# Four more weight remainders on GpSimd, idle products before the first ones, layer norm sums added on Vector, and one key join moved up

## The chip, the cores and the metric

The kernel runs on one core of a Trainium2 chip. TensorE multiplies, Vector and Scalar (rows: DVE and ACT) do the elementwise work, GpSimd (POOL) does some of it, and SyncE (SP) issues nearly all transfers. The metric is the device time of one execution in microseconds.

## The reference

Two transformer blocks of width 2048 on one sequence of 256 tokens, in float32. The change lies in the first half of the first block:

```python
h = rms_norm(x, mix_norm_g)
proj = h @ w_in
q, kv, gate_logits, conv_in = jnp.split(proj, splits, axis=-1)
attn = nsa_attention(q, kv, gates, ...)        # compressed, selected and window branches
# conformer_conv:
a, gate = jnp.split(conv_in, 2, axis=-1)
u = a * jax.nn.sigmoid(gate)
u = causal_depthwise_conv(u, conv_w, conv_b)   # 31 taps, 1024 channels
u = layer_norm(u, ln_g, ln_b)                  # mean and variance over the 1024 channels
conv = jax.nn.silu(u)
x = x + jnp.concatenate([attn, conv], axis=-1) @ w_out
```

Behind it come a gated feed-forward layer with a convolution, and a second block (latent attention, gated linear attention, feed-forward), which the change leaves alone.

## The kernel before

**Products and weights.** Every float32 number a is taken apart as a_hi + a_lo (a_hi rounded for TensorE's fast float32 format), and a product is w_hi*h_hi + w_hi*h_lo + w_lo*h_hi. A planner (`make_plan`) cuts all weights into chunks of 128 x 1024 numbers (512 KB) in the order of use. SyncE loads chunks into 7 raw slots; Scalar rounds a chunk to w_hi (L1193); Vector subtracts to make the remainder w_lo (L1675); TensorE multiplies. w_hi and w_lo have 4 slots, so a chunk can be rounded when the products of the fourth chunk before it are through, and a raw slot is loaded again when the remainder is made. `p.pool_rate` gives the remainders of a stretch of chunks to GpSimd (L2473): from the fifth chunk up to the fourth query tile. `lead(i)` is the third chunk behind chunk i: Scalar and Vector go on rounding and subtracting up to there (`round_until`, `rests_until`) before they turn to the result of the tile that ends in chunk i.

**Order of work.** Each engine has one program, written out by hand, and works it off in order; semaphores tie them together. Scalar squares the rows of x (two tiles of 128 tokens), GpSimd makes the factor of each row (L2477, L2480), and Vector scales x by it in quarters of 512 columns (L1695: quarter 0 of both token tiles, quarter 1 of both, quarters 2 and 3 ahead of k=2 and k=6 of the next step). For each k of 16, TensorE transposes two blocks (L711), Scalar makes h_hi (L1225), and Vector h_lo (L1732). The first pair of tiles, `conv_first`, consists of four chunks of four k's each: for each k two hi products of 512 columns (L617), and at the end of a chunk its eight w_lo products of 256 columns (L618). Transposes run four k's ahead of products.

**Tiles.** 128 output columns each: 16 of the convolution's input, 4 of the compressed keys and values, 8 queries, the gates (48 columns), 4 keys: (1,0), (1,1), (2,0), (2,1); then the value group (two k's for each chunk). A tile's low half is copied out by Scalar (`split_low`, L1258), and Vector adds it (`join_low`, `join_scaled`, L1845). Below, chunks are named by what they hold: K6 holds the last six pieces of key (2,0) and the first two of (2,1), V0, V1 and V2 are the first three of the values.

**Convolution and its layer norm.** Vector runs the 31 taps of eight channel tiles, two tiles at a time (`conv_taps`, L1793, L1796), in portions between its other work: `taps(n)` does the next n instructions, and what is left when the queries are joined is done then. The norm needs sums over 1024 channels, which is eight tiles of 128 partitions: TensorE adds them all with a matrix of ones, eight products on conv_y behind the gates (L811) and eight on the squares behind the tile of key (1,1) (L819). Between the two sums Scalar makes the mean (behind the rounding of chunk K6, L1292), Vector centres (L1887), Scalar squares (L1295). Then follow the root, its refinement, the scaling by it, Scalar's swish (L1312), rounding to mix_hi and the rest mix_lo. The first attention scores (L833) wait for key (2,1), whose join on Vector stands behind the remainders of V1 and V2:

```python
def join_scaled(key, i, dst, scale, done_sem):
    rests_until(lead(final[key]))
    w.wait_ge(low_split, i + 1)
```

TensorE's side of the two sums:

```python
for j in range(CONV_TILES):
    w.wait_ge(taps_done, j + 1)
    t = e.matmul(banks[7][:, 0:T], ones, conv_y[:, j, :], start=j == 0, stop=j == CONV_TILES - 1)
```

`keep_busy` issues products whose result nobody reads, so that TensorE doesn't stand idle while x is normed; it does so ahead of the second, third and fourth h, not of the first.

Of the kernel before, what the change touches and what calls it, by code (L numbers as in the profile page):

```python
# [137 lines left out]
def make_plan():  # L138
# [3 lines left out]
    conv = gates + N_BRANCH * HEADS  # L142
    p.project_pair("conv_first", ("conv_a", 0), ("conv_g", 0), "w_in", (conv, conv + CONV_CH), P)
    p.pool_rate = 1.0
# [151 lines left out]
def two_blocks(nc, WEIGHTS, X, PARAMS, PARAMS1, PARAMS2, POSITIONS, COND, FINAL_ROW, OUT):  # L296
# [12 lines left out]
    with ctx:  # L309
# [122 lines left out]
        low = place("low", "mid", 0, [P, 2, T])  # L432
        sig = place("sig", "mid", (KD + KD // 2) * T * 4 + 2048, [P, 2, T])
# [57 lines left out]
        IDLE_PRODUCTS = ((0, 0), (10, 0), (15, 5), (17, 4))  # L491
# [5 lines left out]
        def sem(name):  # L497
            return ctx.enter_context(nc.semaphore(name))
# [21 lines left out]
        low_split, low_joined = sem("low_split"), sem("low_joined")  # L520
        pads_ready, conv_g_ready, conv_in, taps_done = sem("pads_ready"), sem("conv_g_ready"), sem("conv_in"), sem("taps_done")
# [60 lines left out]
        def tensor_program(e):  # L582
# [112 lines left out]
            def keep_busy(stage, number):  # L695
                if number:
                    src = (None, mix_hi, ff_hi, mix_hi)[stage]
                    b = (None, 5, 2, 2)[stage]
                    fill(b)
                    for _ in range(number):  # L700
                        e.matmul(banks[b][:, :], src[:, 0, 0:P], src[:, 0:2, :].rearrange("p k t -> p (k t)"), start=True, stop=True)
# [34 lines left out]

            w.wait_ge(gains_landed, 16)
# [46 lines left out]
            wide_tile("gates", need, (gates_T_ready, 1), NG)  # L784
            def compressed_scores():
# [22 lines left out]
            fill(7)  # L808
            for j in range(CONV_TILES):
                w.wait_ge(taps_done, j + 1)  # L810
                t = e.matmul(banks[7][:, 0:T], ones, conv_y[:, j, :], start=j == 0, stop=j == CONV_TILES - 1)  # L811
            t.then_inc(ln_summed, 1)
            free[7] = ln_mean_ready, 1
            for at_key, (br, j) in enumerate(((1, 1), (2, 0), (2, 1))):
                if at_key == 1:
                    fill(7)
                    for i in range(CONV_TILES):
                        w.wait_ge(squared, i + 1)
                        t = e.matmul(banks[7][:, 0:T], ones, ln_sq[:, i, :], start=i == 0, stop=i == CONV_TILES - 1)  # L819
                    t.then_inc(ln_summed, 1)  # L820
                    free[7] = ln_var_ready, 1
# [1901 lines left out]
```

## Time and profile before

| | |
|---|---|
| time, median of 3 runs | 2220.71 us (2220.49 to 2220.9) |
| the profiled execution's own time | 2220.59 us |
| its span | 2218.8 us |
| TensorE busy | 2188.2 us (99%) |
| Vector busy | 1574.1 us (71%) |
| Scalar busy | 1123.3 us (51%) |
| GpSimd busy | 128.3 us (6%) |

Busy time of TensorE is the time from the start of a matmul to its modelled end; matmuls overlap, so the spacing of their starts says what one costs. In the timeline a row stands for one or several equal instructions in a row (x8); its first number is the start of the first in us from the span's start, its second the time to the end of the last. What stands in square brackets is how long the engine had been idle and what ended that.

### The profile page before, as it was taken

The numbers are of one execution on the slowest core, as the hardware profiler recorded it, in microseconds if no ns is written. First come the engines' busy times: TensorE is split into PE (matmuls) and PEld (weight loads), VectorE is DVE, ScalarE is ACT, GpSimd is POOL, SyncE is SP. The second block draws the span as 40 slices with busy tenths as digits, with TensorE's granted clock in tenths as the row PEclk, the third lists the DMA queues.
The fourth block names the chain that finished last, engine by engine and source line by source line (L and its number), as shares of the span: only waits on it lengthen the run. The fifth ranks groups of instructions, "written<-read, shape, count | busy, mean of one in ns | idle before, by whom it ended". The sixth has DMA issues, their size and how long they took to land.

```text
span 2218.8 us, 29547 instructions
## 1 busy us (share of the span) xinstructions
PE 2188.2 (99%) x11637; PEld 1853.1 (84%) x11637; DVE 1574.1 (71%) x2417; ACT 1123.3 (51%) x1683; POOL 128.3 (6%) x92
## 2 busy tenths in 40 slices
PE   7999999999999999999999999999999999999998
PEld 6888787888888888888889887878888888888986
DVE  5896886899998799998875665576555555544455
ACT  5444775555543455554455656554444444444443
POOL 5850000000000000000000000000000000000000
PEclk9999999999999999999999999999999999999999
DMA  7754436788899888889955551647676776655563
GB/s 265 225 190 149 135 99 207 245 291 286 292 313 369 308 281 289 290 286 373 338 169 180 177 175 55 233 140 248 230 221 227 227 233 233 214 192 189 182 214 118
DMA packets 139915, 504.00 MB, mean 227 GB/s; under 512 B 15616, under 2 KB 18048, under 8 KB 138880
## 3 DMA queue, kind: packets, MB, share of 16 engines
q1 hardware_dynamic: 138960, 496.85, 67.0%
q0 software_dynamic: 528, 3.16, 0.4%
q8 instruction: 92, 1.51, 0.3%
q10 hardware_dynamic: 288, 2.10, 0.3%
q14 instruction: 47, 0.39, 0.1%
HBM read 499.54 MB, written 2.51 MB: 226 GB/s over the span
## 4 chain that ended last, share of the span: by engine, by line
PE 84%; DVE 12%; ACT 2%; issue 1%; DMA 0%; POOL 0%; POOLq 0%; SPq 0%; DVEq 0%; ACTq 0%
PE bank L627 20%; PE both L627 18%; PE bank L617 13%; PE bank L630 10%; PE both L630 9%; PE bank L618 7%; DVE w_lo L1675 5%; DVE raw L1657 2%; PE bank L620 1%; PE bank L622 1%; PE bank L621 1%; ACT ffn_g L1403 1%; ACT ffn_a L1397 1%; PE bank L876 1%; PE both L833 1%
## 5 line engine op out<-in xcount | busy, mean ns | idle before, releaser
L1675 DVE TENSOR_TENSOR w_lo<-raw,w_hi 128x1024 fp32r<-128x1024 f32 x693 | 840.7, 1222 | 449.7 <-ACT w_hi L1193 448.3
L1193 ACT ACTIVATE w_hi<-raw 128x1024 fp32r<-128x1024 f32 x737 | 767.7, 1054 | 616.2 <-PE bank L630 295.2
L617 PE MATMUL bank<-h_both,w_hi 128*128 128x512 f32 x1936 | 495.0, 395 | 2.8 <-DVE h_both L1732 2.8
L617 PEld LDWEIGHTS bank<-h_both,w_hi 128*128 128x128 f32 x1936 | 346.1, 189 | 66.0 <-DVE h_both L1732 4.4
L618 PEld LDWEIGHTS bank<-h_both,w_lo 128*128 128x128 f32 x1936 | 264.7, 190 | 19.1
L618 PE MATMUL bank<-h_both,w_lo 128*128 128x256 f32 x1936 | 272.2, 283 | 0.0
L1657 DVE SCALAR_TENSOR_TENSOR raw<-raw,silu_c 128x1024 f32<-128x1024 f32 x192 | 234.0, 1219 | 0.0
L627 PE MATMUL bank<-w_hi,h_both 128*128 128x512 f32 (+2 forms) x1024 | 233.9, 372 | 0.0
L627 PE MATMUL both<-w_hi,h_both 128*128 128x512 f32 (+1 forms) x960 | 228.4, 379 | 1.4 <-DVE h_both L1752 1.4
L627 PEld LDWEIGHTS bank<-w_hi,h_both 128*128 128x128 f32 x1024 | 181.9, 188 | 33.1 <-issue 0.7
L627 PEld LDWEIGHTS both<-w_hi,h_both 128*128 128x128 f32 x960 | 169.3, 188 | 33.9 <-DVE h_both L1752 2.8
L630 PE MATMUL bank<-w_lo,h_both 128*128 128x512 f32 (+2 forms) x512 | 126.4, 371 | 0.0
L630 PE MATMUL both<-w_lo,h_both 128*128 128x512 f32 (+1 forms) x480 | 120.7, 375 | 0.0
L627 PE MATMUL bank<-w_hi,ff_hi 128*128 128x512 f32 x352 | 111.0, 389 | 0.0
L627 PE MATMUL bank<-w_hi,ff_lo 128*128 128x512 f32 x352 | 110.9, 389 | 0.0
L627 PE MATMUL both<-w_hi,ff_hi 128*128 128x512 f32 x352 | 108.7, 390 | 1.0 <-ACT w_hi L1193 1.0
L627 PE MATMUL both<-w_hi,ff_lo 128*128 128x512 f32 x352 | 108.4, 389 | 0.0
L2473 POOL TENSOR_TENSOR w_lo<-raw,w_hi 128x1024 fp32r<-128x1024 f32 x44 | 104.9, 2408 | 39.6 <-ACT w_hi L1193 38.7
L630 PEld LDWEIGHTS bank<-w_lo,h_both 128*128 128x128 f32 x512 | 91.4, 188 | 16.2
L630 PEld LDWEIGHTS both<-w_lo,h_both 128*128 128x128 f32 x480 | 86.3, 188 | 16.4
L630 PE MATMUL bank<-w_lo,ff_hi 128*128 128x512 f32 x352 | 95.4, 389 | 0.0
L630 PE MATMUL both<-w_lo,ff_hi 128*128 128x512 f32 x352 | 94.1, 389 | 0.0
(369 smaller groups left out, 2343.9 us busy)
## 6 DMA issues: line engine op xcount, KB each, us to landing
raw<-weights SPq DMA_DIRECT2D x924, 512.0 KB, 4.5
raw<-weights SPq DMA_DIRECT2D x5, 504.0 KB, 7.3
x<-x SPq DMA_DIRECT2D x2, 1024.0 KB, 5.8
bias<-bias_rows SPq DMA_DIRECT2D x8, 256.0 KB, 6.8
silu_c<-c ACTq DMA_DIRECT2D x2, 1024.0 KB, 4.7
gate_row<-gate_rows POOLq DMA_DIRECT2D x2, 1024.0 KB, 9.0
out<-x SPq DMA_DIRECT2D x8, 256.0 KB, 2.7
final_row<-final_row POOLq DMA_DIRECT2D x1, 1024.0 KB, 5.2
```

What stands on the lines that cost most here:

```text
L617: return e.matmul(out, hi, a_both[:, k, :, :].rearrange("p a t -> p (a t)"), start=first, stop=last)
L618: return e.matmul(out[:, 0:T], lo, a_hi[:, k, :], start=False, stop=False)
L620: e.matmul(out, hi, a_hi[:, k, :], start=opens and first, stop=False)
L621: return e.matmul(out, hi, a_lo[:, k, :], start=False, stop=False)
L622: return e.matmul(out, lo, a_hi[:, k, :], start=False, stop=closes and last)
L627: t = e.matmul(outs[o], stationary[:, k, o * P:(o + 1) * P], hi, start=opens and first and stationary is a_hi, stop=False)
L630: t = e.matmul(outs[o], a_hi[:, k, o * P:(o + 1) * P], lo, start=False, stop=closes and last)
L833: t = e.matmul(both[:, side, br * n:(br + 1) * n], queries[r, j, tt * P:(tt + 1) * P], keys[r, br, j // GQA, 0:n], start=True, stop=True)
L1193: e.activation(w_hi[:, n % PART_SLOTS, 0:widths[i]], raw[:, i % RAW_SLOTS, 0:widths[i]], ACT.Copy).then_inc(hi_ready, 1)
L1657: e.scalar_tensor_tensor(src, src, 1.0, silu_c[:, half, :], ALU.mult, ALU.mult, accum_out=ada_parts[:, v, kt, half:half + 1]).then_inc(ada ...
L1675: e.tensor_tensor(w_lo[:, slot, 0:widths[i]], raw[:, i % RAW_SLOTS, 0:widths[i]], w_hi[:, slot, 0:widths[i]].bitcast(F32), ALU.subtract).t ...
L2473: e.tensor_tensor(w_lo[:, slot, 0:widths[i]], raw[:, i % RAW_SLOTS, 0:widths[i]], w_hi[:, slot, 0:widths[i]].bitcast(F32), ALU.subtract).t ...
```

## The change

Four parts. (1) `pool_rate` is set before the first chunk, so GpSimd makes the remainders of chunks 0 to 3 as well; Vector makes none of them. (2) Vector clears a small tile, `blank`, and TensorE runs 8 products on it at once, 10 when the first half of x has landed, 5 between the first two transposes, and 2 when the first four k's are transposed. (3) Vector adds the eight tiles of conv_y, and later the eight tiles of squares, into one tile of 256 columns (ln_q); TensorE then needs one product with the matrix of ones for each sum. The first seven additions are put into `conv_taps`, behind each pair of channel tiles; the second seven stand behind the centring and the remainder of the next chunk, K6. (4) Scalar splits and Vector joins key (2,1) before the last chunks of its lead (V1 and V2) are subtracted (on Scalar: before V2 is rounded).

```diff
     conv = gates + N_BRANCH * HEADS
+    p.pool_rate = 1.0
     p.project_pair("conv_first", ("conv_a", 0), ("conv_g", 0), "w_in", (conv, conv + CONV_CH), P)
-    p.pool_rate = 1.0
     for j in range(1, CONV_TILES):
...
         low = place("low", "mid", 0, [P, 2, T])
+        blank = place("blank", FR, 0, [P, 512], BF16)
         sig = place("sig", "mid", (KD + KD // 2) * T * 4 + 2048, [P, 2, T])
...
         WITH_H = (WITH_PAIR, WITH_PAIR, WITH_GROUP, WITH_GROUP)
-        IDLE_PRODUCTS = ((0, 0), (10, 0), (15, 5), (17, 4))
+        WARM_PRODUCTS = (8, 10)
+        IDLE_PRODUCTS = ((5, 2), (10, 0), (15, 5), (17, 4))
         TURN_BANKS = ((6, 7, 0, 1), (6, 7, 0, 1), (6, 7, 4, 5), (6, 7, 4, 5))
...
                 if number:
-                    src = (None, mix_hi, ff_hi, mix_hi)[stage]
-                    b = (None, 5, 2, 2)[stage]
+                    b = (2, 5, 2, 2)[stage]
                     fill(b)
                     for _ in range(number):
-                        e.matmul(banks[b][:, :], src[:, 0, 0:P], src[:, 0:2, :].rearrange("p k t -> p (k t)"), start=True, stop=True)
+                        if stage == 0:
+                            e.matmul(banks[b][:, :], blank[:, 0:P], blank[:, :], start=True, stop=True)
+                        else:
+                            src = (mix_hi, ff_hi, mix_hi)[stage - 1]
+                            e.matmul(banks[b][:, :], src[:, 0, 0:P], src[:, 0:2, :].rearrange("p k t -> p (k t)"), start=True, stop=True)
 
...
 
+            w.wait_ge(dve_step, 1)
+            keep_busy(0, WARM_PRODUCTS[0])
+            w.wait_ge(x_landed[0], 16)
+            keep_busy(0, WARM_PRODUCTS[1])
             w.wait_ge(gains_landed, 16)
...
             wide_tile("gates", need, (gates_T_ready, 1), NG)
+            def norm_sum(added, taken):
+                w.wait_ge(norm_added, added)
+                fill(7)
+                e.matmul(banks[7][:, 0:T], ones, ln_q[:, :], start=True, stop=True).then_inc(ln_summed, 1)
+                free[7] = taken, 1
+
             def compressed_scores():
...
                 free[2 + tt] = gates_ready, tt + 1
-            fill(7)
-            for j in range(CONV_TILES):
-                w.wait_ge(taps_done, j + 1)
-                t = e.matmul(banks[7][:, 0:T], ones, conv_y[:, j, :], start=j == 0, stop=j == CONV_TILES - 1)
-            t.then_inc(ln_summed, 1)
-            free[7] = ln_mean_ready, 1
+            norm_sum(1, ln_mean_ready)
             for at_key, (br, j) in enumerate(((1, 1), (2, 0), (2, 1))):
                 if at_key == 1:
-                    fill(7)
-                    for i in range(CONV_TILES):
-                        w.wait_ge(squared, i + 1)
-                        t = e.matmul(banks[7][:, 0:T], ones, ln_sq[:, i, :], start=i == 0, stop=i == CONV_TILES - 1)
-                    t.then_inc(ln_summed, 1)
-                    free[7] = ln_var_ready, 1
+                    norm_sum(2, ln_var_ready)
                 wide_tile(("key", br, j), need, (keys_ready, at_key + 2))
...
             for at_key, (br, j) in enumerate(((1, 1), (2, 0), (2, 1))):
-                split_low(made(("key", br, j)), 30 + at_key, ((low_joined, 21), (keys_ready, 1), (keys_ready, 2))[at_key])
+                if at_key == 2:
+                    round_until(final["key", br, j])
+                    w.wait_ge(multiplied, done_at["key", br, j])
+                    split_low(banks[bank_of["key", br, j]], 32, (keys_ready, 2))
+                    round_until(lead(final["key", br, j]))
+                else:
+                    split_low(made(("key", br, j)), 30 + at_key, ((low_joined, 21), (keys_ready, 1))[at_key])
                 if at_key == 0:
...
 
+            chain(e.memset(blank[:, :], 0.0))
             for parts, value in ((out1_parts, D * EPS), (final_parts, D * EPS), (product_parts, 0.0), (o2_raw_parts, D * EPS),
...
             def conv_taps():
-                before = {}
+                before, last_tap = {}, {}
                 for j0 in range(0, CONV_TILES, 2):
...
                                 if j >= 2:
-                                    w.wait_ge(taps_done, j - 1)
+                                    w.wait_ge(dve_step, last_tap[j - 2])
                                 before[j] = chain(e.tensor_scalar(so_far, u, tap_w, conv_b[:, j:j + 1], ALU.mult, ALU.add))
...
                                 w.wait_ge(dve_step, before[j])
-                                e.scalar_tensor_tensor(conv_y[:, j, :], u, tap_w, so_far, ALU.mult, ALU.add).then_inc(taps_done, 1)
+                                last_tap[j] = chain(e.scalar_tensor_tensor(conv_y[:, j, :], u, tap_w, so_far, ALU.mult, ALU.add))
                             yield
+                    w.wait_ge(dve_step, last_tap[j0 + 1])
+                    if j0 == 0:
+                        so_far_y = chain(e.tensor_tensor(ln_q[:, :], conv_y[:, 0, :], conv_y[:, 1, :], ALU.add))
+                        yield
+                        continue
+                    for j in (j0, j0 + 1):
+                        w.wait_ge(dve_step, so_far_y)
+                        t = e.tensor_tensor(ln_q[:, :], ln_q[:, :], conv_y[:, j, :], ALU.add)
+                        if j < CONV_TILES - 1:
+                            so_far_y = chain(t)
+                        else:
+                            t.then_inc(norm_added, 1)
+                        yield
 
...
             def join_scaled(key, i, dst, scale, done_sem):
-                rests_until(lead(final[key]))
+                rests_until(lead(final[key]) if i < 32 else final[key])
                 w.wait_ge(low_split, i + 1)
...
             for j in range(CONV_TILES):
-                w.wait_ge(taps_done, j + 1)
                 e.tensor_tensor(conv_y[:, j, :], conv_y[:, j, :], ln_mean[:, :], ALU.subtract).then_inc(centred, 1)
+            rests_until(lead(final["key", 1, 0]) + 1)
+            w.wait_ge(squared, 2)
+            t = chain(e.tensor_tensor(ln_q[:, :], ln_sq[:, 0, :], ln_sq[:, 1, :], ALU.add))
+            for j in range(2, CONV_TILES):
+                w.wait_ge(squared, j + 1)
+                w.wait_ge(dve_step, t)
+                if j < CONV_TILES - 1:
+                    t = chain(e.tensor_tensor(ln_q[:, :], ln_q[:, :], ln_sq[:, j, :], ALU.add))
+                else:
+                    e.tensor_tensor(ln_q[:, :], ln_q[:, :], ln_sq[:, j, :], ALU.add).then_inc(norm_added, 1)
             rests_until(lead(final["key", 1, 1]))
...
             join_scaled(("key", 2, 1), 32, keys[:, 1, 1, :], 1.0, keys_ready)
+            rests_until(lead(final["key", 2, 1]))
             for j in range(CONV_TILES):
```

## Rows read from the trace of the kernel before

**Rows 1.** The page, chain that ended last: shares of the span by engine.
```profile
PE 84%; DVE 12%; ACT 2%; issue 1%; DMA 0%; POOL 0%; POOLq 0%; SPq 0%; DVEq 0%; ACTq 0%
```

**Rows 2.** Windows by stage; columns: stretch, busy time (instructions) of each engine, clock, DMA share, GB/s.
```profile
60.00:80.00 20.00, 20.00 (x115) 17.58 (x114) 17.02 (x44) 9.68 (x13) 16.77 (x8) 1.00 1.02 270
200.00:250.00 50.00, 49.01 (x255) 40.70 (x255) 40.07 (x74) 35.30 (x70) 0.00 (x0) 1.00 0.43 131
```

**Rows 3.** Timeline of TensorE, 9 to 31 us: start, duration, engine, line, operation, tiles, count, wait.
```profile
11.84 0.90 PE L711 MATMUL bank<-lasting,wide 128*128 128x128 f32 x3 [2.03 <-DVE wide L1695]
14.16 1.22 PE L617 MATMUL bank<-h_both,w_hi 128*128 128x512 f32 x2 [0.57 <-DVE h_both L1732]
15.46 1.20 PE L617 MATMUL bank<-h_both,w_hi 128*128 128x512 f32 x2
21.51 0.73 PE L617 MATMUL bank<-h_both,w_hi 128*128 128x512 f32 x2 [0.52 <-DVE h_both L1732]
22.21 0.71 PE L617 MATMUL bank<-h_both,w_hi 128*128 128x512 f32 x2
22.76 1.11 PE L618 MATMUL bank<-h_both,w_lo 128*128 128x256 f32 x8
```

**Rows 4.** Timeline of Vector in the same stretch.
```profile
11.30 1.28 DVE L1695 TENSOR_SCALAR wide<-x,stat 128x512 f32<-128x512 f32 x3 [2.08 <-POOL stat L2480]
12.50 1.22 DVE L1675 TENSOR_TENSOR w_lo<-raw,w_hi 128x1024 fp32r<-128x1024 f32 x1
13.63 0.87 DVE L1732 SCALAR_TENSOR_TENSOR h_both<-bank,lasting,h_both 128x256 fp32r<-128x256 f32 x2
```

**Rows 5.** GpSimd's L2473 and L2477 (ns min/median/max), and timeline near 1125, 1171 us.
```profile
L2473 POOL TENSOR_TENSOR w_lo<-raw,w_hi x44: 2368/2407/2429, 24.0 to 153.4; 128x1024 fp32r<-128x1024 f32 x44
...
L2477 POOL TENSOR_SCALAR stat<-stat x14: 186/192/487, 7.8 to 1358.6; 128x1 f32<-128x1 f32 x14
...
1125.36 1.33 POOL L2497 DMA_DIRECT2D gate_rows<-lasting  x1
1125.84 1.07 DVE L1690 TENSOR_SCALAR wide<-x,stat 128x512 f32<-128x512 f32 x1
...
1171.03 0.49 DVE L2100 TENSOR_SCALAR c_q<-c_q,stat 128x512 f32<-128x512 f32 x1 [1.00 <-POOL stat L2480]
1171.08 0.49 POOL L2477 TENSOR_SCALAR stat<-stat 128x1 f32<-128x1 f32 x1
```

**Rows 6.** Timeline of the two norm sums, 200 to 213 us.
```profile
200.38 3.72 PE L811 MATMUL bank<-conv_y,lasting 128*128 128x256 f32 x16
...
203.75 0.81 PE L617 MATMUL bank<-h_both,w_hi 128*128 128x512 f32 x2
...
206.26 2.78 DVE L1887 TENSOR_TENSOR conv_y<-conv_y,ln_mean 128x256 f32<-128x256 f32 x8 [3.79 <-ACT ln_mean L1292]
...
212.80 0.81 PE L617 MATMUL bank<-h_both,w_hi 128*128 128x512 f32 x2
```

**Rows 7.** Timeline of Vector: its wait before the gates, and two dependent instructions.
```profile
191.48 0.42 DVE L1813 TENSOR_TENSOR bank<-bank,low 48x256 f32<-48x256 f32 x1 [4.72 <-ACT low L1258]
...
221.79 0.42 DVE L1912 TENSOR_TENSOR ln_q<-ln_q,ln_rs 128x256 f32<-128x256 f32 x1
...
222.25 0.43 DVE L1914 SCALAR_TENSOR_TENSOR ln_rs<-ln_q,ln_rs 128x256 f32<-128x256 f32 x1
```

**Rows 8.** Timeline before the first scores.
```profile
226.10 2.06 ACT L1312 ACTIVATE conv_y<-conv_y,phase 128x256 f32<-128x256 f32 x4
...
228.70 1.07 PE L630 MATMUL bank<-w_lo,h_both 128*128 128x512 f32 x4
...
230.76 0.71 PE L833 MATMUL both<-keys,queries 64*128 64x128 f32 x8 [0.99 <-DVE keys L1845]
```

**Rows 9.** Windows at the end of the kernel, columns as in Rows 2.
```profile
2210.00:2212.00 2.00, 0.02 (x1) 0.00 (x0) 1.81 (x4) 0.72 (x2) 0.23 (x1) 1.00 0.71 208
2212.00:2213.00 1.00, 0.00 (x0) 0.00 (x0) 0.49 (x2) 0.00 (x0) 0.70 (x1) 0.53 0.69 260
```

More of the change, by code:

```diff
@@ L519, in two_blocks @@
         attended, attn_rounded, attn_ready = sem("attended"), sem("attn_rounded"), sem("attn_ready")
-        low_split, low_joined = sem("low_split"), sem("low_joined")
-        pads_ready, conv_g_ready, conv_in, taps_done = sem("pads_ready"), sem("conv_g_ready"), sem("conv_in"), sem("taps_done")
+        low_split, low_joined, norm_added = sem("low_split"), sem("low_joined"), sem("norm_added")
+        pads_ready, conv_g_ready, conv_in = sem("pads_ready"), sem("conv_g_ready"), sem("conv_in")
         ln_summed, ln_mean_ready, centred, squared, tile_done = sem("ln_summed"), sem("ln_mean_ready"), sem("centred"), sem("squared"), sem("tile_done")
```

## The prediction

> **What bounds the kernel now.** I read the shares of the chain of waits first (84% TensorE, 12% Vector [rows 1]), then the windows by stage, then the timeline of the two places that the change touches. From 31 us to the end of the query tiles TensorE is busy without a gap [rows 2], the other engines are not: whatever starts this stretch earlier or later moves everything behind it by the same amount. Transfers only follow the release of their slots and were far from full between 200 and 250 us [rows 2], so they move along. Two places are left in which time can be won or lost: the start (up to 31 us) and the stretch from the last query to the first attention scores (186 to 231 us).
>
> The start. The products of k=0 begin at 14.16, two products and two transposes take 1.30 us there (14.16 to 15.46), and 0.70 us later on (21.51 to 22.21) [rows 3]. The clock column shows full speed for this stretch, but 512 columns in 0.43 us are the lower level, 1.2 GHz, and 0.23 us the upper one; TensorE had been idle up to its transposes at 11.84, and reached the fast pace about 16.9. Vector is in the way too: the remainder of h for k=0 is ready for it about 12.8, but waits behind the weight remainder of 12.50 to 13.72 [rows 4], and h for k=6 comes 0.52 us late [rows 3]. From the second set of w_lo products, 22.76, nothing waits for Vector any more, so I measure the start by how that row moves.
>
> **What the change does, step by step.**
>
> *Start, remainders.* Four Vector subtractions of 1.22 us go to GpSimd, where one takes 2.41 us [rows 4, 5]. GpSimd finishes them about 13.8, 16.5, 18.8 and 21.2; TensorE would want them about 16.9, 19.8, 23.5 and 26.0, so their length is hidden. Raw slots are released within 0.5 us of before.
>
> *Start, warm products.* 8 products on the blank tile run from about 1.2 us (8 x 0.43 = 3.4 us), 10 from 5.7, 5 behind the first transpose. They end before the transposes at 11.84, which wait for x, and their cover is that idle time. Before, the fast pace came 5 us after TensorE's first steady work, so it should be there by 11.84. The memset of the blank tile lies where Vector waits for x.
>
> If nothing stood against it: h for k=0 at 13.2; then 0.68 us for each k with transposes, 0.45 for the last four, 0.95 for 8 w_lo products, and one wait of 0.35 us at k=2, where Scalar's rounding of chunk 1 comes in between. That puts the second w_lo set at 19.8: 2.9 us earlier. With the slow clock as before it would be 1.0 us earlier.
>
> *Start, what stands against it.* The eight scalings of x (L1695, 0.48 us each [rows 4]) now lie beside GpSimd's remainders. The trace shows such neighbours: a one-column GpSimd instruction of 0.19 us takes 0.49 us beside a Vector scaling of 0.49 us and ends with it, and Vector's second scaling at 1125.84 takes 1.07 instead of 0.48 us beside a GpSimd DMA issue [rows 5]. So the two engines shut each other out, and GpSimd got in between two back-to-back scalings. How long a Vector scaling waits for a 2.41 us GpSimd subtraction no row shows: all 44 of them took 2.37 to 2.43 us, beside Vector instructions that read PSUM. The lower bound is nothing. The upper one is all of it: the scaling (1,0) waits for chunk 0's remainder (11.8 to 14.2), (1,1) for chunk 1's (14.7 to 17.1), then h of k=0 at 17.5 and its products at 18.0; (2,0) waits for chunk 2's, (3,0) for chunk 3's, and the second w_lo set starts at 26.2, 3.5 us late; with TensorE idle from 13 to 18 its clock is low again, and it is 4.6. Between the ends I take the row that is nearest in kind, 0.59 us for a meeting (1.07 less 0.48), at three meetings (before k=0, k=2 and k=6): 1.8 us. Start: -2.9 + 1.8 = -1.1 us. If Vector kept its place over a run of scalings and only then waited, it would come out alike, at -1.3.
>
> The Trainium skill states this as a lock: "Whoever issues first gets the shared pair for the whole instruction; the other **fully blocks**" (SBUF — State Buffer, Who interferes with whom). By that rule the start is the upper bound, 3.5 to 4.6 us late; the trace agrees as to GpSimd waiting for Vector (0.49 us), and does not show the other way with a long instruction.
>
> *First norm sum.* Eight products on conv_y take 3.37 us on TensorE (200.38 to 203.75), one takes 0.42 [rows 6]: 2.9 us less. The seven additions go behind the taps of each pair. As taps are given out by number, about eight steps are left behind the last query (one before): 3.5 us in Vector's idle time of 4.72 us before 191.48 [rows 7]. The sum is ready about 190, ten us early. The five additions beside GpSimd's remainders can meet them too, 2.4 us each at most; a tile's bank is wanted again only two tiles (5.6 us) later, so I put them at nothing.
>
> *Second norm sum.* The same on TensorE, but its seven additions lie on the path. Moved up by 2.9 us, the mean lets the centrings start at 203.3 (206.26 before), and their 2.78 us end at 206.1 [rows 6]; then the remainder that now stands before the additions (1.22), to 207.2; then seven dependent additions at 0.46 us, the spacing of two dependent instructions in [rows 7], to 210.4. TensorE starts the tile of key (1,1) at 200.8 and is through at 206.7. It waits 3.8 us. The next tile starts at 210.84 instead of 212.80: 1.96 us earlier, where without the wait it would be 5.9.
>
> *Key join.* Everything from the root to the swishes follows TensorE and comes 1.96 us earlier. The swishes end at 226.1 instead of 228.1 [rows 8], the low half of key (2,1) is split right behind them, one rounding earlier than before, and joined at 226.5 to 226.9. But now chunk V1's remainder stands behind this join, not ahead: it comes 226.85 to 228.1, and TensorE, 1.96 us ahead of 228.70, wants it at 226.8. Its w_lo products, 228.70 before, start at 228.1, and the first scores right behind them at 229.05 instead of 230.76, without the 0.99 us wait of before [rows 8]. Vector has its last remainder 1.5 us earlier than before and makes the second unit wait for that: 1.5 us remain.
>
> *The clock in the 3.8 us wait.* At the end of the kernel the granted clock fell between 2212 and 2213 us, two to three us behind the last product [rows 9]. So I let it fall here. If it is back 5 us after it fell, as at the start, some 3.2 us of products run at half speed: 1.6 us lost. Bounds: nothing, and 2.5 us (5 us at half speed). This stretch: -1.5 + 1.6 = +0.1.
>
> Sum: -1.1 + 0.1 = -1.0 us, against the profiled execution's own 2220.59 (span 2218.8 and 1.8 around it), 0.1 us from the median of 2220.71. That is 2219.6, so 2219.5 rounded. Within 0.2% (4.4 us) a measurement of this kernel can hardly tell it from no change.
>
> **The rivals.**
>
> *The full lock (ends on the other side).* Place: scalings (1,0), (1,1), (2,0), (3,0). Price: start +3.5 to +4.6, with the second stretch +0.1 a total of 2224.2 to 2225.3; if the clock stays up in the second wait, 2222.6 at the least, and if it stays down for 5 us, 2226.2. It is slower beyond the bound from a start of +4.5 on. For it: GpSimd got in between two scalings, and everything in GpSimd's row looks like exclusive use. Against it: no long GpSimd instruction is seen to hold Vector up.
>
> *No meeting costs anything.* Start -2.9, total 2217.8; with the clock kept up in the 3.8 us wait 2216.2, just faster beyond the bound. For it: the 44 remainders never vary. Against it: the 1.07 us scaling.
>
> *The additions are hidden, too.* If the seven additions end when TensorE comes, the two sums give 5.9 us and the join up to 1.0: 2211 to 2214 with any start up to 0. Against it: mean, centring and squares lie in a row, and 0.46 us is what a dependent instruction costs.
>
> *The warm products warm nothing,* since the clock falls again before 11.84 or blank operands don't count: start 1.9 us later than summed (1.0 gained in place of 2.9), 2221.4. For it: at the end it fell within two to three us. Against it: no gap between them is longer than 1.3 us.
>
> **Chances.** Forecast (part of a remainder is waited for, 2218 to 2221) 0.34; full lock 0.32; no meeting 0.22; warm products without effect 0.07; hidden additions 0.05. Range: from the no-meeting case with a kept clock, 2216.2, to the full lock, 2225.3; some 2 in 10 lie outside, half of it above. The likeliest one's own range is 2217.5 to 2221.5. Faster beyond 0.2% (below 2216.3): a quarter of no meeting, the hidden additions, a little of the forecast: 0.14. Slower (above 2225.1): over half of the full lock and a little else: 0.22. Within: 0.64.
>
> **What would show it.** In the start: the durations of the eight scalings (0.48 each if there is no meeting, 1.07 by the forecast, up to 2.9 by the lock), the start of the first L617 product (13.3, 13.9, 18.0), that of the second L618 set (19.8, 21.6, 26.2 or later), and the spacing of the first transposes. In the second stretch: one product for each sum, TensorE idle for 3.8 us behind the tile of key (1,1), the next tile at 210.8 when moved by the start's shift, products of 0.23 or 0.43 us behind it, and TensorE waiting for V1's remainder instead of for the keys. The prediction is wrong if the second wait is under 2 us, if the pair is held for whole remainders, or if a bank is late behind a tap addition.

## The result, and the profile after

The changed kernel takes 2224.11 us in the median of 20 runs (2222.89 to 2225.18), the kernel before 2220.68 (2220.41 to 2221.35) in as many: a ratio of 1.0015, interval 1.0009 to 1.0022. So it is 3.4 us slower, where 1.2 us faster was forecast. The size is within the 0.2% of "no change" and inside the range, the sign is not the one forecast. The profiled execution took 2224.11 itself, with a span of 2222.3. The shares of the chain of waits are the same as before [rows 1].

The start first. Timeline of TensorE, columns as in [rows 3]:

```profile
11.82 0.55 PE L716 MATMUL bank<-lasting,wide 128*128 128x128 f32 x3 [0.26 <-DVE wide L1706]
12.64 0.59 PE L703 MATMUL bank<-blank 128*128 128x512 bf16 x2
17.20 1.13 PE L619 MATMUL bank<-h_both,w_hi 128*128 128x512 f32 x2 [3.96 <-DVE h_both L1743]
18.41 1.20 PE L619 MATMUL bank<-h_both,w_hi 128*128 128x512 f32 x2
21.09 0.70 PE L619 MATMUL bank<-h_both,w_hi 128*128 128x512 f32 x2
25.30 0.87 PE L620 MATMUL bank<-h_both,w_lo 128*128 128x256 f32 x6
```

The transposes run at the fast pace (0.55 us for three, 0.90 in [rows 3]), so the idle products had brought the clock up. Then TensorE waits 3.96 us for h, and the first products take 1.13 and 1.20 us a pair, the slow pace again. The windows' granted clock is 0.58 from 17 to 19 us. The second set of w_lo products starts at 25.30, 2.54 us later than in [rows 3] (the view ends at 26 us and so counts six of its eight). What h waited for stands in the timelines of Vector's scalings (L1706, the old L1695):

```profile
11.28 0.49 DVE L1706 TENSOR_SCALAR wide<-x,stat 128x512 f32<-128x512 f32 x1 [2.08 <-POOL stat L2515]
...
11.68 2.58 DVE L1706 TENSOR_SCALAR wide<-x,stat 128x512 f32<-128x512 f32 x1
...
14.18 2.57 DVE L1706 TENSOR_SCALAR wide<-x,stat 128x512 f32<-128x512 f32 x1
...
17.46 1.79 DVE L1706 TENSOR_SCALAR wide<-x,stat 128x512 f32<-128x512 f32 x1
19.17 0.47 DVE L1706 TENSOR_SCALAR wide<-x,stat 128x512 f32<-128x512 f32 x1
```

and of GpSimd's remainders (L2508, the old L2473):

```profile
11.35 2.63 POOL L2508 TENSOR_TENSOR w_lo<-raw,w_hi 128x1024 fp32r<-128x1024 f32 x1
...
14.05 2.42 POOL L2508 TENSOR_TENSOR w_lo<-raw,w_hi 128x1024 fp32r<-128x1024 f32 x1
...
16.43 2.53 POOL L2508 TENSOR_TENSOR w_lo<-raw,w_hi 128x1024 fp32r<-128x1024 f32 x1
...
21.57 2.68 POOL L2508 TENSOR_TENSOR w_lo<-raw,w_hi 128x1024 fp32r<-128x1024 f32 x1 [2.61 <-ACT w_hi L1198]
```

Put side by side, the two engines take turns. The scaling at 11.68 meets the remainder that runs to 13.98, and ends at 14.26; the next meets the one that runs to 16.47, and ends at 16.75; that at 17.46 meets the one to 18.96, and ends at 19.25. Each ends about 0.28 us behind the remainder. The pair at 11.28 shows the other direction: the remainder takes 2.63 us in place of 2.41 beside a scaling.

The second stretch. Timeline of TensorE around the two sums (L797 is the sum's product), and of Vector:

```profile
202.93 0.70 PE L797 MATMUL bank<-ln_q,lasting 128*128 128x256 f32 x2
203.32 0.76 PE L619 MATMUL bank<-h_both,w_hi 128*128 128x512 f32 x2
...
208.83 0.39 PE L619 MATMUL bank<-h_both,w_hi 128*128 128x512 f32 x1
213.26 1.22 PE L797 MATMUL bank<-ln_q,lasting 128*128 128x256 f32 x2 [4.04 <-DVE ln_q L1921]
213.92 1.41 PE L619 MATMUL bank<-h_both,w_hi 128*128 128x512 f32 x2
...
215.56 3.46 PE L619 MATMUL bank<-h_both,w_hi 128*128 128x512 f32 x8
```

```profile
205.79 2.77 DVE L1911 TENSOR_TENSOR conv_y<-conv_y,ln_mean 128x256 f32<-128x256 f32 x8 [0.77 <-ACT ln_mean L1297]
208.48 1.22 DVE L1686 TENSOR_TENSOR w_lo<-raw,w_hi 128x1024 fp32r<-128x1024 f32 x1
209.61 0.42 DVE L1914 TENSOR_TENSOR ln_q<-ln_sq 128x256 f32<-128x256 f32 x1
210.13 2.54 DVE L1919 TENSOR_TENSOR ln_q<-ln_q,ln_sq 128x256 f32<-128x256 f32 x5
212.78 0.42 DVE L1921 TENSOR_TENSOR ln_q<-ln_q,ln_sq 128x256 f32<-128x256 f32 x1
```

In the windows (columns as in [rows 2]) the granted clock, 1.00 there before, is down:

```profile
210.00:215.00 5.00, 1.74 (x4) 1.46 (x5) 4.34 (x10) 2.13 (x3) 0.00 (x0) 0.69 0.40 108
215.00:220.00 5.00, 5.00 (x20) 4.17 (x20) 2.88 (x7) 0.85 (x1) 0.00 (x0) 0.63 0.41 141
```

The first sum gives what was forecast: its tile starts at 203.32, 0.43 us earlier than in [rows 6] although the start is 2.54 late. The second takes more than that back. And the first scores come 3.80 us later than in [rows 8], behind a wait for V1's remainder instead of for the keys. Timelines of TensorE and Vector:

```profile
233.42 1.21 PE L632 MATMUL bank<-w_lo,h_both 128*128 128x512 f32 x4 [1.22 <-DVE w_lo L1686]
234.56 0.71 PE L838 MATMUL both<-keys,queries 64*128 64x128 f32 x8
```

```profile
231.80 0.42 DVE L1870 SCALAR_TENSOR_TENSOR keys<-bank,low 128x256 f32<-128x256 f32 x1 [2.65 <-ACT low L1263]
232.14 2.35 DVE L1686 TENSOR_TENSOR w_lo<-raw,w_hi 128x1024 fp32r<-128x1024 f32 x2
```

Of these 3.80 us the start has 2.54 and this stretch 1.26; the spans differ by 3.5.

### The profile page after: what moved, and what is told of

Its sections match the earlier page's. It is cut to its first block, busy times and chain, and to the rows that moved or that the text cites. A ratio compares the mean times of both kernels' runs of the same rounds, so it can differ in the third digit from the quotient of the medians.

```text
span 2222.3 us, 29555 instructions
## 1 busy us (share of the span) xinstructions
PE 2193.9 (99%) x11634; PEld 1852.0 (83%) x11634; DVE 1580.7 (71%) x2428; ACT 1123.3 (51%) x1683; POOL 138.5 (6%) x96
## 4 chain that ended last, share of the span: by engine, by line
PE 84%; DVE 12%; ACT 2%; issue 1%; DMA 0%; POOL 0%; POOLq 0%; DVEq 0%; SPq 0%; ACTq 0%
PE bank L629 20%; PE both L629 18%; PE bank L619 13%; PE bank L632 10%; PE both L632 9%; PE bank L620 7%; DVE w_lo L1686 5%; DVE raw L1668 2%; PE bank L622 1%; PE bank L624 1%; PE bank L623 1%; ACT ffn_a L1408 1%; ACT ffn_g L1414 1%; PE bank L881 1%; PE both L838 1%
## 5 line engine op out<-in xcount | busy, mean ns | idle before, releaser
L1686 DVE TENSOR_TENSOR w_lo<-raw,w_hi 128x1024 fp32r<-128x1024 f32 (+1 forms) x689 | 835.6, 1222 | 448.7 <-ACT w_hi L1198 447.2
L2508 POOL TENSOR_TENSOR w_lo<-raw,w_hi 128x1024 fp32r<-128x1024 f32 x48 | 115.2, 2421 | 31.9 <-ACT w_hi L1198 30.8
```

The costliest lines, as they stand in the source:

```text
L1686: e.tensor_tensor(w_lo[:, slot, 0:widths[i]], raw[:, i % RAW_SLOTS, 0:widths[i]], w_hi[:, slot, 0:widths[i]].bitcast(F32), ALU.subtract).t ...
L2508: e.tensor_tensor(w_lo[:, slot, 0:widths[i]], raw[:, i % RAW_SLOTS, 0:widths[i]], w_hi[:, slot, 0:widths[i]].bitcast(F32), ALU.subtract).t ...
```

## The experiments

Times are medians of 11 runs; the kernel before took 2220.62, 2220.57, 2220.72 and 2220.65 us in the four sets, in this order.

**The parts alone.** `pool_only` is the kernel before with the remainders of the first four chunks on GpSimd:

```diff
+    p.pool_rate = 1.0
     p.project_pair("conv_first", ...)
-    p.pool_rate = 1.0
```

> The kernel before, with the remainders of chunks 0 to 3 on GpSimd and nothing else of the change. Theory E (Vector's scalings of x and GpSimd's remainders shut each other out for whole instructions, each taking turns): the scalings (1,0), (1,1) and (2,0) take 2.6, 2.6 and about 1.8 us, the first products of conv_first start at 17.2 or a little later, the second set of w_lo products at 25.3 (22.76 before), total 2223.2 (+2.5). Theory R (the late start comes from the idle products or from GpSimd's remainders being late themselves, the scalings only show it): the scalings keep 0.48 us, the start is within 0.5 us of before or earlier, total 2220 to 2221.

Measured: 2223.14 us (2222.91 to 2225.49), ratio 1.0014, interval 1.0005 to 1.0023. This part alone costs 2.5 us. The scalings' line (ns min/median/max), 472 to 490 ns without such neighbours:

```profile
L1695 DVE TENSOR_SCALAR wide<-x,stat x8: 474/782/2583, 8.7 to 22.1; 128x512 f32<-128x512 f32 x8
```

The time is the expected one, the places are not. Four scalings meet a remainder (2.58, 1.81, 2.57 and 1.08 us), and each again ends 0.28 us behind it. Scaling (1,1) slips through, since chunk 1 isn't rounded yet, and so the first products start at 15.04 (17.2 expected) and the second set at 24.99, 2.23 us later than in [rows 3]. Here TensorE waits 2.08 us, and the products behind the wait are fast:

```profile
20.06 0.74 PE L617 MATMUL bank<-h_both,w_hi 128*128 128x512 f32 x2 [2.08 <-DVE h_both L1732]
```

`warm_only` is the kernel before with the blank tile and its idle products.

> The kernel before, with the idle products on the blank tile and nothing else. Both theories: the fast pace is there at 11.84, but Vector's remainder of chunk 0 still stands before h of k=0, so the first products start at 14.2 as before and the second set of w_lo products at about 22.7: total 2220.7, no change (2220.2 to 2221.2). If the warm products were a cost by themselves, over 2221.5.

Measured: 2220.6 us (2220.48 to 2220.71), ratio 1.0, interval 0.9991 to 1.0008: nothing. TensorE's timeline shows why. Its last idle products end about 13.1, h comes 0.91 us later, and the first real products are slow all the same (0.73 us would be the fast pace; the granted clock is 0.50 from 15 to 17 us). The length of the gap alone doesn't explain it: the transposes of the same run come behind a gap of 1.06 us and are fast.

```profile
11.71 0.55 PE L716 MATMUL bank<-lasting,wide 128*128 128x128 f32 x3 [1.06 <-DVE wide L1704]
...
12.53 0.59 PE L703 MATMUL bank<-blank 128*128 128x512 bf16 x2
14.03 1.17 PE L619 MATMUL bank<-h_both,w_hi 128*128 128x512 f32 x2 [0.91 <-DVE h_both L1741]
```

`sums_join` is the changed kernel with the start of before: only the norm sums and the key join are changed.

> The change without its two parts at the start: only the norm sums on Vector and the moved join. By the trace after, this stretch comes 1.3 us later at the first scores, of which 2.2 us are the slow clock behind TensorE's 4 us wait. So 2221.9 in the executions in which the clock stays low that long (2220 to 2222.5 over all, with a spread of about 2 us between executions, where the kernel before has 0.9). The rival (all of the loss is the start's): 2219 to 2219.5, spread as before.

Measured: 2221.05 us (2220.54 to 2221.99), ratio 1.0002, interval 0.9993 to 1.0011. The whole second part is worth +0.4 us, within what can be told from nothing; the wait for the second sum is 4.04 us here too. Its second set of w_lo products started at 23.28 us, with the start of the kernel before (22.76 in [rows 3]): single executions of the same start differ by half a microsecond.

`odd_scales` is the changed kernel with scalings of 513 and 511 columns in turn.

```diff
-cols = slice(n * 512, (n + 1) * 512)
+cols = slice(n * 512 + n % 2, (n + 1) * 512 + (n + 1) % 2)
```

> The changed kernel, with the scalings of x cut at odd columns (513, 511, 513, 511 in place of four times 512), same arithmetic. Theory E in the form that only Vector's faster two-port form of a scaling shuts GpSimd out, and needs an even count: each scaling takes about 0.60 us and meets nothing, the GpSimd remainders take 2.41, the first products start at about 13.6, the second set of w_lo products at about 20.1 (25.3 with even widths), total 2219 (5 us under the changed kernel). If any Vector instruction beside a GpSimd one waits, or if the start is late for another reason: no difference, 2224.

Measured: 2223.93 us (2222.85 to 2225.11), ratio 1.0014, interval 1.0006 to 1.0023, as the changed kernel. The scalings without a neighbour still took 0.49 us, so the odd widths didn't make them another kind of instruction; they meet the remainders as in the changed kernel (three scalings in 5.48 us in both), and the run doesn't tell which kind would escape. It was a bad test. The Trainium skill would have said so (VectorE: DVE Perf Modes, What auto-detection actually checks): for the fast form the outer sizes of source and destination may be even or equal, and these are equal.

**Where the remainders meet the scalings.** `pool_wait` keeps GpSimd's remainders back until the eight scalings are done, and makes quarter 3 right behind quarter 2.

```diff
 # GpSimd, ahead of each remainder
+w.wait_ge(scaled, 8)
 # Vector, rest_h
-if k in (2, 6):
-    scale_quarter(scale, 2 + k // 4, early)
+if k == 2 and stage == 0:
+    scale_quarter(scale, 2, early)
+    scale_quarter(scale, 3, early)
+elif k in (2, 6) and stage:
+    scale_quarter(scale, 2 + k // 4, early)
```

> The changed kernel, with two differences at the start: GpSimd's remainders wait until all eight scalings are done, and Vector makes the scalings of quarters 2 and 3 one after the other before the third h_lo. Theory (the whole loss at the start is scalings held behind whole GpSimd remainders): every scaling takes 0.47 to 0.49 us again, GpSimd's first remainder starts at about 15.1 us and the first three end at about 17.5, 19.9 and 22.3; the second set of w_lo products starts at 20.4 to 21.5 us instead of 25.30, and the time falls by 3.5 to 4.5 us from the changed kernel's 2224.1, to 2219.6 to 2220.6. Rival (GpSimd's remainders are by themselves too slow for the start, 2.4 us against Vector's 1.2 us, whatever the scalings do): the second set starts at 23.5 us or later and no more than 1.5 us comes back, 2222.6 or more.

Measured: 2219.43 us (2219.26 to 2220.39), ratio 0.9996, interval 0.9987 to 1.0004: 4.7 us less than the changed kernel, with the same work on each engine. The scalings' line, then TensorE's timeline:

```profile
L1706 DVE TENSOR_SCALAR wide<-x,stat x8: 477/481/489, 8.7 to 14.7; 128x512 f32<-128x512 f32 x8
```

```profile
13.28 0.73 PE L619 MATMUL bank<-h_both,w_hi 128*128 128x512 f32 x2
...
17.72 1.21 PE L620 MATMUL bank<-h_both,w_lo 128*128 128x256 f32 x8 [0.66 <-POOL w_lo L2512]
...
21.52 1.12 PE L620 MATMUL bank<-h_both,w_lo 128*128 128x256 f32 x8
```

The second set starts 1.24 us earlier than in [rows 3] and 3.78 us earlier than in the changed kernel. The other 0.9 us of the 4.7 lie in the second stretch. From the last row ahead of the wait for the second sum to the row behind the slow products (205.06 to 215.08, in the changed kernel 208.83 to 219.80) pass 10.02 us instead of 10.97, though the wait is 4.04 us in both: the slow products end sooner. Nothing ties these 0.9 us to the remainders. Two things were changed here, the wait and the place of quarter 3; neither was run by itself. In this execution the idle products and the first real ones are fast.

`cold_wait` is the same without the idle products.

> The changed kernel with GpSimd's first remainders held back until the scalings are done, and without the idle products. Theory (the idle products matter little, since what TensorE has to do before 17.7 us is waited for on GpSimd's first remainder anyway): the first products take 1.2 us for a pair again instead of 0.73, the first set of w_lo products starts at 17.7 to 18.3 us instead of 17.72, and the time is 2219.4 to 2220.1. Rival (with the scalings out of the way TensorE bounds the start, and the lower clock goes straight into the time): the first set starts at 18.6 us or later, and the time is 2220.5 to 2221.5.

Measured: 2219.52 us (2219.33 to 2220.91), ratio 0.9996, interval 0.9987 to 1.0005. The idle products are worth about 0.1 us even where they work: the slow products end before GpSimd's first remainder is there.

```profile
13.34 1.22 PE L619 MATMUL bank<-h_both,w_hi 128*128 128x512 f32 x2
...
17.81 1.22 PE L620 MATMUL bank<-h_both,w_lo 128*128 128x256 f32 x8 [0.41 <-POOL w_lo L2507]
```

**The second stretch, one thing at a time.** `first_sum` is the kernel before with the first norm sum by additions and nothing else.

> The kernel before with nothing of the change but the first norm sum made by Vector's additions and one TensorE product (no idle products, no remainders moved to GpSimd, the second sum as eight products, the keys' join where it was). Theory (the first sum's additions hide in Vector's idle time and its products' 2.9 us of TensorE come back whole): the tile behind the first norm sum starts 2.9 us earlier, and the time falls by 2.5 to 3.1 us, to 2217.5 to 2218.2. Rival (the scores' wait for the keys, or Vector's joins behind, take part of it back): 1 to 2 us, 2218.7 to 2219.7.

Measured: 2217.57 us (2217.44 to 2218.8), ratio 0.9987, interval 0.9978 to 0.9996. All of it lasts, 3.08 us, and the scores wait for the keys as before (0.99 us):

```profile
200.44 0.70 PE L793 MATMUL bank<-ln_q,lasting 128*128 128x256 f32 x2
...
227.80 0.71 PE L839 MATMUL both<-keys,queries 64*128 64x128 f32 x8 [0.99 <-DVE keys L1864]
```

`old_second` is the changed kernel with the second sum as eight products on the squares, as before.

```diff
 # TensorE; Vector's seven additions are taken out as well
-norm_sum(2, ln_var_ready)
+fill(7)
+for i in range(CONV_TILES):
+    w.wait_ge(squared, i + 1)
+    t = e.matmul(banks[7][:, 0:T], ones, ln_sq[:, i, :], ...)
...
```

> The changed kernel with the second norm sum made as before (eight TensorE products with the ones matrix, no additions on Vector); the first sum stays with the additions. Theory (the second sum's additions cost more than the products that they replace, by the wait of 4.04 us and by the clock behind it): the next tile starts about 1.5 us earlier beside the end of the tile before it, the granted clock stays at 1.00 from 210 to 220 us, and TensorE is 3 to 3.7 us ahead when it comes to chunk V1; how much of that lasts depends on V1's remainder, so 2220.5 to 2223.0 in all. Rival (the end of the stretch is set by Vector, with the joins and V1's remainder, and what TensorE saves becomes a longer wait in front of V1, now 1.22 us): 2223.5 to 2224.1.

Measured: 2221.02 us (2219.97 to 2221.68), ratio 1.0001, interval 0.9992 to 1.0009: 3.1 us less than the changed kernel, and the clock stays at 1.00 in every window from 205 to 225.

`filled_wait` is the changed kernel with 16 idle products ahead of the second sum's product.

```diff
+fill(7)
+if added == 2:
+    for _ in range(16):
+        e.matmul(banks[7][:, :], h_hi[:, 0, 0:P], h_both[:, 0, :, :]..., start=True, stop=True)
 w.wait_ge(norm_added, added)
-fill(7)
```

> The changed kernel with 16 idle products of 128x512 ahead of the second norm sum's one product, so that TensorE doesn't rest while Vector adds; they use h_hi and write the norm sum's bank before the sum starts it anew. Theory (2.2 us of the loss is the granted clock that falls in the wait): the clock stays at 1.00 from 210 to 220 us, the products behind the norm sum keep their 0.22 us spacing, TensorE comes to V1 2.2 us earlier; 2222.0 to 2223.5 in all. Rival (V1's remainder takes the gain as a longer wait): within 0.5 us of the changed kernel, 2223.6 to 2224.6.

Measured: 2222.45 us (2221.56 to 2222.75), ratio 1.0007, interval 0.9998 to 1.0016: 1.7 us less than the changed kernel. In the profiled execution the start came out 0.85 us later than in the changed kernel's, so the stretch itself gave more, 2.5 us (209.68 to 218.12, 8.44 us between the rows that were 10.97 apart). The remaining wait is short, and the eight products that took 3.46 us take 1.99:

```profile
214.11 0.70 PE L800 MATMUL bank<-ln_q,lasting 128*128 128x256 f32 x2 [0.39 <-DVE ln_q L1924]
...
215.34 1.99 PE L619 MATMUL bank<-h_both,w_hi 128*128 128x512 f32 x8
```

`join_v1` is the changed kernel with key (2,1) joined behind V1's remainder.

```diff
-rests_until(lead(final[key]) if i < 32 else final[key])
+rests_until(lead(final[key]) if i < 32 else groups["value"][2][0])
```

> The changed kernel with the join of key (2,1) put behind the remainder of chunk V1 in Vector's order, and ahead of V2's. Theory (the join that was moved up now holds up V1's remainder, and TensorE waits 1.22 us for it): the wait in front of V1 shrinks by 0.6 to 1.2 us, the scores start at 233.4 to 234.0 instead of 234.56, and the time falls by 0.5 to 1.2 us. Rival (the scores wait for the keys instead, as they did before the change, where that wait was 1.0 us): within 0.3 us of the changed kernel.

Measured: 2223.36 us (2222.07 to 2224.66), ratio 1.0012, interval 1.0003 to 1.0021: 0.75 us less. The wait for V1 is gone (the scores start at 232.91, earlier than expected), and half of it comes back ahead of the second unit:

```profile
237.19 1.13 PE L838 MATMUL both<-keys,queries 64*128 64x256 f32 x8 [0.62 <-DVE scores L1969]
```

**Better versions.** `best` puts `pool_wait`, `old_second` and `join_v1` together.

> The changed kernel with three of the differences tried so far together: GpSimd's first remainders behind the eight scalings, the second norm sum as eight TensorE products, and key (2,1) joined behind V1's remainder. Theory (the three losses are separate): 2219.43 us with the first, less 2.5 to 3.1 us for the second sum (the whole wait of 4.04 us and the granted clock behind it, against 3.26 us of products), less 0.7 us for the join, 2215.6 to 2216.3. Rival (they hide one another, because the end of the stretch is set by Vector): 2217.5 or more.

Measured: 2215.84 us (2215.72 to 2216.12), ratio 0.9978, interval 0.9969 to 0.9987, 4.9 us faster than the kernel before. By the medians the three savings add: 2224.11 - 4.68 - 3.09 - 0.75 = 2215.59. That fit is in part chance, as 0.9 us of the 4.68 were won on slow products behind a wait that `best` doesn't have. And its start, the same edits as in `pool_wait`, ran with a slow clock in the profiled execution: the transposes, the idle products and the first product are slow, although no gap lies ahead of that product.

```profile
11.92 0.90 PE L716 MATMUL bank<-lasting,wide 128*128 128x128 f32 x3 [1.11 <-DVE wide L1711]
...
13.97 1.41 PE L619 MATMUL bank<-h_both,w_hi 128*128 128x512 f32 x2
```

`sum_inside` keeps the additions of the second sum and puts its product inside the tile of key (2,0):

```diff
+def summing():
+    for _ in range(26):
+        yield
+    norm_sum(2, ln_var_ready)
+    yield
...
-wide_tile(("key", br, j), need, (keys_ready, at_key + 2))
+wide_tile(("key", br, j), need, (keys_ready, at_key + 2), beside=in_tile)
```

> As the last, but the second norm sum stays with Vector's additions and its one product is put inside the tile of key (2,0), behind 26 of its 32 products' places, so that TensorE has that tile's products to make while Vector adds. Theory (the additions are nearly free where TensorE needn't wait for them): against the version with GpSimd held back (2219.43 us) the wait of 4.04 us goes, the clock stays at 1.00 (1.6 us there), and the join gives 0.7 us: 2212.5 to 2214. Rival (Vector's seven additions make the remainder of the tile's later chunk late, 213.12 us in the changed kernel, and TensorE waits for that instead): 2 us or more of it is given back, 2215 to 2217.

Measured: 2215.79 us (2215.6 to 2216.32), ratio 0.9978, interval 0.9969 to 0.9986, the same as `best`. TensorE no longer waits for the sum, but 1.8 to 3.3 us of the hoped-for gain are missing. The rival had the time right and the place wrong (TensorE waits at V1 and at the second unit, not for the tile's later chunk):

```profile
210.08 0.60 PE L797 MATMUL bank<-ln_q,lasting 128*128 128x256 f32 x2
...
221.88 2.12 PE L629 MATMUL bank<-w_hi,h_both 128*128 128x512 f32 x8 [2.17 <-ACT w_hi L1205]
...
229.61 1.14 PE L845 MATMUL both<-keys,queries 64*128 64x256 f32 x8 [1.12 <-DVE scores L1979]
```

Scalar's rounding of V1 stands behind four swishes, and these wait 3.51 us for Vector's scaling by the root. By this trace Vector's chain behind the additions then sets the pace of the stretch; no run shortened that chain to show it.

## Why the prediction was wrong

**The failed step** is the price of the scalings beside GpSimd's remainders: "0.59 us for a meeting", at three meetings 1.8 us. There were three meetings, and they cost 2.10, 2.09 and 1.31 us (scalings of 2.58, 2.57 and 1.79 us in place of 0.48), 5.5 us in all. What happened is nearly the upper bound, named there with its places. The forecast put the start at -1.1; it came out at +2.54 in the trace, and `pool_only` at +2.5 us in the time. The full-lock rival had given +3.5 to +4.6. It was too high, first, because the first products started at 17.20 and not at 18.0, and then because the fourth remainder started only at 21.57, when its raw chunk had been rounded, and no scaling waited for it (quarter 3's took 0.87 us for two, from 21.14).

`pool_wait` shows the cause: with the same remainders on the same engine, moved off the scalings in time, every scaling takes 0.48 to 0.49 us again and the second w_lo set comes 3.8 us earlier. The row taken as nearest in kind, the scaling of 1.07 us beside a DMA issue, was read by its excess and not by its end. The issue ended at 1126.69 (1125.36 and 1.33 in [rows 5]) and the scaling at 1126.91, 0.22 us behind it. So 0.59 us was no fixed price: it goes by what was left of a 1.33 us instruction. Behind a 2.41 us one the same reading gives nearly the upper bound: what a meeting costs is the rest of whatever is running. (It is one row, and the scaling ahead of it took its usual 0.49 us though it began behind the issue's start.)

The Trainium skill has this rule (SBUF — State Buffer, Who interferes with whom), and the rows now agree: 2.58 us for 0.48 us of work. By that rule the forecast would have been the rival's 2224.2 to 2225.3 us, beside the measured 2224.11. That it is so near is partly luck: the start came out 1 us under the rival's and the second stretch 1.2 us over.

**The warm products.** The prediction counted 1.9 us for them and gave 0.07 to their being without effect. They did warm TensorE for the transposes, but the first real products were slow behind the wait of 3.96 us, and in `warm_only` behind one of 0.91 us. So this rival was right in size, 0.0 us alone. Its first reason, that the clock falls again, was right too: later than at 11.84 in the changed kernel and `warm_only`, and already at 11.92 in the trace of `best`. What decides it between one execution and the next is open; it isn't the gap alone. In the trace of `pool_wait` the clock was up, and that gave 0.1 us against `cold_wait`, since TensorE waits for GpSimd there.

**First norm sum.** Right: -2.9 forecast, -3.08 measured by itself. The sum was ready at 192.2, more than ten us ahead of its use; with the shift of the start 192.5 was forecast. That its additions can meet GpSimd's remainders was put at nothing. Only one of the seven started well inside a remainder, and it was held like the scalings: 0.64 us in place of 0.42, ending 0.28 us behind the remainder. Nothing waited for it.

```profile
146.46 2.39 POOL L2508 TENSOR_TENSOR w_lo<-raw,w_hi 128x1024 fp32r<-128x1024 f32 x1
...
148.49 0.64 DVE L1817 TENSOR_TENSOR ln_q<-ln_q,conv_y 128x256 f32<-128x256 f32 x1
```

**Second norm sum.** Mechanism right, sizes a little off. The wait was 4.04 us (3.8 forecast): the additions follow one another at 0.53 us, not 0.46, and take 3.6 us. The next tile came 1.42 us earlier against the shifted start (1.96 forecast). The forecast's own numbers made the second sum's additions a loss of 2.5 us (2.9 us ahead before it, 1.96 behind it, and 1.6 for the clock), but it never set them against leaving this sum alone: eight products cost 3.26 us of TensorE (209.54 to 212.80 in the kernel before) and no wait, and the kernel takes 3.1 us more with the additions than with the eight products (`old_second`).

**The clock in that wait.** Right as a step, under-sized: 1.6 us forecast. From the next tile to the row that is 3.66 us behind it in the kernel before, 5.88 pass now (213.92 to 219.80), 2.2 us more. `filled_wait` gives 1.7 us in the time. The term varies between executions: the eight products that took 3.46 us took 2.66 in `sums_join` and 3.55 in `pool_wait`, each behind a wait of 4.04 us. It is not the only thing that spreads the times, though. The changed kernel's range is 2.3 us (0.9 for the kernel before), but `pool_only`, which has no such wait, ranges over 2.6 us, and with the start of the changed kernel the second w_lo set stood at 25.21 us in one trace (`join_v1`) and at 26.12 in another (`filled_wait`).

**Key join.** Right in kind: the wait for the keys went, and a wait for V1 came, 1.22 us (1.3 forecast). `join_v1` prices it at 0.75 us, since the second unit takes the rest. The stretch as a whole was forecast at +0.1; it was +1.26 in this trace and +0.4 in the time of `sums_join`.

The terms measured one by one add up: +2.5 (remainders) - 3.1 (first sum) + 3.1 (second sum) + 0.75 (join) = +3.3, against +3.4 measured. Part of this is chance, for grouped otherwise they differ by some 0.5 us: the changed kernel is 3.1 us slower than `sums_join`, which lacks its start, where the remainders alone cost 2.5; and `sums_join` is at +0.4, where the last three terms give +0.75.

## What to carry to other kernels

Before work is given to an idle engine, list what the other engine does in that time and look in the trace for the two of them together; where a pair ends at the same time, price a meeting at the whole remaining length of the longer instruction, and let the long ones wait until the short ones on the critical path are done. An addition chain on Vector is free in place of TensorE's products only if its operands are ready early: the first sum, needed ten us later, gained 3.1 us, and the second, the same edit with its operands just made, lost 3.1. A wait of TensorE of about 4 us cost its own length and 1.4 to 2.5 us of slow products behind it (estimates from the rows around it in six traces, 9.86 to 10.97 us beside the 8.44 of `filled_wait`); waits of 2.08 and 2.17 us (`pool_only`, `sum_inside`) had fast products behind them.

## What the runs showed of the hardware

- Vector's scaling of 128x512 float32 numbers and GpSimd's subtraction of 128x1024 take turns by whole instructions: 0.48 us became 2.58, and the scaling ended 0.28 us behind the subtraction each time. GpSimd got its turn between two scalings issued back to back (11.28 and 11.68), and Vector between two subtractions. The 0.48 us of a scaling were unchanged at odd widths.
- A Vector addition of two 128x256 tiles was held by the same subtraction in the same way: 0.42 us became 0.64, and it ended 0.28 us behind. The other six began less than 0.1 us before a subtraction ended, or while none ran, and took 0.41 or 0.42 us. Vector's scalar_tensor_tensor for h_lo, which reads PSUM, took 0.47 us inside a subtraction (17.07 us).
- Products were slow 0.91 us after idle products had ended (`warm_only`), and fast behind gaps of 1.06 (transposes, same run), 2.08 and 2.17 us. In the six traces with a wait of 4.04 us for the second sum they were slow each time. With the same start edits and idle products the start was fast in `pool_wait` and slow in `best`. What sets this from execution to execution no run here isolates.
- In the kernel before, the windows' clock column says 1.00 from 10 to 20 us, while a pair of products takes 1.2 us up to 16.7; only the spacing shows the clock of that start.
